# A dense value product for prompt tiles 1 and 2 of a product-key expert layer, with the expert value table read once

## The chip, the cores and the metric

The program runs on 1 core of one Trainium2 chip. Its time is the device time of one execution in microseconds, the median of several runs. Before the change it is 2445.83 us, the median of 3 runs.

## What is computed

The kernel is one decoder layer for a prompt of 512 tokens (with 16 meta tokens ahead of it) and 64 sample tokens (8 sequences of 8, each over 2048 cached keys). It projects, attends in two ways (a sparse attention with an indexer, and a forgetting attention), merges, normalises, and then runs the expert layer that the change is about. All data is float32.

```python
# peer, for one token x (1024 values), 8 heads, two sets of 128 keys a head
experts = ...            # 8 x 16 numbers in 0..16383, = 128*row + column, the best key pairs
gate = softmax(top)      # over the 16 of a head
pre = einsum('thkd,td->thk', expert_u[experts], x)
coef = gate * gelu(pre)
return einsum('thk,thkd->td', coef, expert_v[experts])
```

So each token needs its own 128 rows of `expert_u` and its own 128 rows of `expert_v`, both tables of 16384 rows of 1024 values (4 KB a row, 67 MB a table). After it, `x = LN2(ALPHA * h + PEER(h))`.

## The kernel before

Everything is written for the five engines by hand, with semaphores. The first 450 us or so are the projections and the prompt's attention. After them all engines follow one list, `plan`, built in Python: 1152 row gathers in a fixed order, and every other piece of work put at the number of a gather (`put(n, ...)`). Each engine walks through the list in order and does its own pieces, so a wait in one piece holds up everything that the same engine has behind it in the list.

Tokens come in five tiles: tiles 0 to 3 are prompt tiles of 128 tokens, tile 4 is the 64 sample tokens. A gather is an indirect DMA of GpSimd (line 918) that brings 128 table rows (512 KB) into one row buffer.

- U gathers (key rows, `expert_u`). One brings one expert row for each of a tile's 128 tokens, so a prompt tile needs 128 of them, and tile 4, packed two picks at a time, 64. VectorE multiplies the buffer with the tokens' h and sums (line 2081), which gives one column of `pre`.
- V gathers (value rows, `expert_v`). One brings the 128 rows of one token. TensorE multiplies them with the token's 128 coefficients, which ScalarE has laid into a strip (`add_rows`, line 1369): two matmuls of 512 columns with a 32-column stationary operand. The token's place in the strip decides its output row. A prompt tile has four such 32-column lanes, which TensorE can work at together when four tokens' rows are there (a `sum` of size 4). Each matmul is two instructions in the trace, since it is float32. Sums of one token stand where V gathers alternate with U gathers.

The order of gathers before: U of tile 0 (128), 72 V of tile 0, U of tile 1 mixed with the other 56 V of tile 0, then U of tiles 2, 3 and 4 mixed with V of earlier tiles, and last V of tile 4 (64). There are 10 row buffers (`NR0`), and 16 from gather 790 on. A gather waits for the product or sum that last read its buffer.

Beside the gathers the list carries: the routing of each tile on VectorE (16 steps of `route`, the best 16 keys and pairs a head), `gelu` and `coefs`, two merges (TensorE with weights that SyncE loads), and the sample attention: `ix`, `iy` (indexer products over pages that SyncE loads), `admit`, 32 rounds of `top` on VectorE (lines 1967 and 1968, 8 keys a round), and eight quarters `s_score`, `s_max`, `s_exp`, `s_turn`, `s_weigh`, `s_out` over cached keys and values (84 MB, SyncE's queue, a ring of four 1 MB slots). Before, `ix` starts at gather 199, `admit` stands at 276, the last `s_out` at 744, and the last merge ends at 840. At a tile's end `finish` adds the sums to h and `y_end` normalises.

## Time and profile before

| | |
|---|---|
| time, median of 3 runs (lowest to highest) | 2445.83 us (2444.44 to 2457.82) |
| span of the profiled execution | 2493.9 us |
| mean granted TensorE clock | 0.853 of full |
| bytes read from HBM | 784.13 MB |
| gathers | 576 of U and 576 of V rows, 604.58 MB |
| busy: TensorE, VectorE, GpSimd | 73%, 57%, 52% |

The profiled execution has no time of its own beside its span, 2493.9 us, which lies 48 us above the median of the plain runs (a factor of 0.981). Shares of busy time are means over stages that have different limits, so they say little about what a change in one stage is worth. "Idle before" in a group is the time in which the engine stood still just before such an instruction.

### The profile page before, as it was taken

Reading aid. Unit: us, or ns where it says so; the run is one execution under the profiler, and the core shown is the slowest. Engines: PE = TensorE matmul, PEld = TensorE weight load, DVE = VectorE, ACT = ScalarE, POOL = GpSimd, SP = SyncE. Lnnn points to the kernel's source line nnn. Section 1 sums busy time; section 2 is a strip of 40 time slices with the busy share of each in tenths; the row PEclk is TensorE's granted clock in tenths of the full one; section 3 lists DMA queues with packets and bytes.
Section 4 is the critical chain, followed back from the end, with each engine's and each line's share of the span. In section 5 each row is a group of like instructions: output and inputs, shape, how many; then the busy total and the mean of one; then the engine's idle time right before and its main releaser. Section 6 shows DMA issues by size and latency. Waiting matters only on the chain.

```text
span 2493.9 us, 23573 instructions
## 1 busy us (share of the span) xinstructions
PE 1810.2 (73%) x7244; PEld 768.0 (31%) x7247; DVE 1433.9 (57%) x3191; ACT 307.8 (12%) x732; POOL 1307.8 (52%) x1175
## 2 busy tenths in 40 slices
PE   9999988899699635566666766776777884555566
PEld 6767646644244201111112121221223250110011
DVE  2115876898845643999856569854444437434400
ACT  0214442111011101001101010110110010000000
POOL 1100000467655744555555557766777747677664
PEclk9998987999899867777778789998999997876678
DMA  5206322999989976999999999999999999999997
GB/s 182 71 3 195 102 85 68 355 328 410 361 306 368 346 281 238 394 367 400 386 401 380 401 371 362 371 356 368 378 384 409 409 370 374 364 359 380 355 377 287
DMA packets 259648, 791.92 MB, mean 318 GB/s; under 512 B 31522, under 2 KB 56163, under 8 KB 258947
## 3 DMA queue, kind: packets, MB, share of 16 engines
q0 software_dynamic: 166400, 604.58, 63.6%
q1 hardware_dynamic: 91268, 180.82, 20.6%
q10 hardware_dynamic: 1856, 5.03, 0.5%
q8 instruction: 58, 0.95, 0.2%
q14 instruction: 66, 0.54, 0.1%
HBM read 784.13 MB, written 5.59 MB: 317 GB/s over the span
## 4 chain that ended last, share of the span: by engine, by line
POOL 13%; DMA 10%; PE 8%; issue 7%; SPq 7%; another core or an unknown queue 6%; DVE 2%; ACT 1%; POOLq 0%
POOL arena L918 13%; DMA arena<-v_b 4%; PE ps L1369 3%; SPq L841 3%; DMA arena<-peer_v,arena 3%; SPq L768 2%; DMA arena<-peer_u,arena 2%; PE ps L1325 2%; DMA arena<-kv_a 2%; SPq L834 1%; PE ps L1202 1%; DVE arena L2081 1%; PE ps L1302 1%; ACT arena L1640 0%
## 5 line engine op out<-in xcount | busy, mean ns | idle before, releaser
L1369 PE MATMUL ps<-arena 128*32 128x512 f32 x2304 | 767.5, 717 | 346.6 <-DMA arena<-peer_v,arena 287.9
L2081 DVE CUSTOM_DVE_ANT_0 arena<-arena 128x1024 f32<-128x1024 f32 x576 | 694.7, 1225 | 531.5 <-DMA arena<-peer_u,arena 475.7
L918 POOL DMA_INDIRECT arena<-peer_v,arena x576 | 623.4, 1082 | 445.9 <-PE ps L1369 245.0
L918 POOL DMA_INDIRECT arena<-peer_u,arena x576 | 664.1, 1153 | 311.8 <-issue 162.2
L1369 PEld LDWEIGHTS ps<-arena 128*32 128x32 f32 x2304 | 153.4, 122 | 877.7 <-issue 662.1
L1164 PE MATMUL ps<-arena 128*128 128x448 f32 (+2 forms) x512 | 156.8, 467 | 13.1 <-DVE arena L1997 12.4
L1202 PE MATMUL ps<-arena 128*128 128x384 f32 (+2 forms) x704 | 146.5, 368 | 10.0 <-ACT arena L1576 8.1
L1325 PE MATMUL ps<-arena 128*64 128x512 f32 (+1 forms) x512 | 102.6, 538 | 68.1 <-DMA arena<-v_b 57.3
L900 POOL MEMSET arena<- 128x1024 f32 x1 | 1.0, 953 | 282.4 <-ACTq L723 282.4
L950 PE MATMUL ps<-arena 128*128 128x296 f32 (+1 forms) x512 | 132.1, 419 | 6.2 <-DMA arena<-xT 6.2
L1699 ACT ACTIVATE arena<-arena 128x8 f32<-128x8 f32 x72 | 15.3, 216 | 943.1 <-PE ps L1369 635.2
L1202 PEld LDWEIGHTS ps<-arena 128*128 128x128 f32 x704 | 104.3, 202 | 58.9 <-issue 26.8
L1164 PEld LDWEIGHTS ps<-arena 128*128 128x128 f32 x512 | 89.0, 193 | 87.0 <-issue 70.4
L950 PEld LDWEIGHTS ps<-arena 128*128 128x128 f32 (+1 forms) x512 | 96.9, 190 | 39.7 <-issue 8.3
L1284 PE MATMUL ps<-arena 128*32 128x512 f32 x256 | 51.6, 901 | 61.3 <-DMA arena<-k_b 61.0
L1325 PEld LDWEIGHTS ps<-arena 128*64 128x64 f32 x512 | 39.7, 159 | 144.0 <-issue 143.2
L895 POOL DMA_INDIRECT arena<-logf_b,arena x16 | 14.6, 913 | 126.4 <-PE ps L950 113.6
L2088 DVE SCALAR_TENSOR_TENSOR arena<-arena,ps 128x1024 f32<-128x1024 f32 (+1 forms) x5 | 6.1, 1219 | 126.2 <-PE ps L1369 84.6
L1967 DVE MAX8 arena<-arena 64x8 f32<-64x2056 f32 x32 | 73.6, 2299 | 1.0
L979 PE MATMUL ps<-arena 64*128 64x384 f32 (+9 forms) x168 | 69.9, 525 | 4.9 <-ACT arena L1545 1.9
L1968 DVE MATCH_REPLACE8 arena<-arena 64x2056 f32<-64x2056 f32 x32 | 73.1, 2286 | 0.0
L1825 DVE MAX8 arena<-arena 128x8 f32<-128x128 f32 (+3 forms) x120 | 34.2, 325 | 58.6 <-ACT arena L1583 53.2
(211 smaller groups left out, 1694.1 us busy)
## 6 DMA issues: line engine op xcount, KB each, us to landing
arena<-k_b SPq DMA_DIRECT2D x128, 256.0 KB
arena<-v_b SPq DMA_DIRECT2D x128, 256.0 KB
arena<-w_mix SPq DMA_DIRECT2D x56, 512.0 KB
arena<-w_q SPq DMA_DIRECT2D x48, 512.0 KB
arena<-kv_a SPq DMA_DIRECT2D x128, 128.0 KB
arena<-w_out SPq DMA_DIRECT2D x24, 512.0 KB
arena<-peer_u,arena POOLq DMA_INDIRECT x576
arena<-peer_v,arena POOLq DMA_INDIRECT x576
```

The lines of the kernel that those rows point to most:

```text
L841: sp.dma_start(ring[s_][:, j * 256:(j + 1) * 256], io["kv_a"][bass.ds(nos[j], 1)].rearrange("o p n -> (o p) n")).then_inc(ring_loaded[s_], 16)
L918: pool.indirect_dma_start(out=rows[slot_of[n]], out_offset=None, in_=io["peer_v"] if v else io["peer_u"], in_offset=bass.IndirectOffsetOnA ...
L950: last = pe.matmul(bank(2 * (m % 2) + a, HT, 0, n), wring[m % 3][:, k, 0:n], xT[:, k, a * HT:(a + 1) * HT], start=(k == 0), stop=(k == KD ...
L979: last = pe.matmul(out, heads[0:rows_, q, q0:q0 + nq], heads[0:rows_, kt, c0:c1], start=True, stop=not biased)
L1164: last = pe.matmul(out, mw_k[u % NMW][:, k0 + k, :], src[:, k, :], start=(k == 0), stop=(k == nk - 1))
L1202: last = pe.matmul(bank(4 + n % 2, WIDTH[p]), mw_k[u % NMW][:, k, :], hT[p][:, k, :], start=(k == 0), stop=(k == KD - 1))
L1284: last = pe.matmul(out[32 * lane:32 * lane + 32], qs_flat[:, at + 32 * lane:at + 32 * lane + 32], kk[e][:, :, hp, :], start=(hp % 2 == 0), ...
L1325: last = pe.matmul(out[e], probT_s[:, c, j * 128 + 64 * e:j * 128 + 64 * e + 64], rhs, start=(c == 0 and j == 0), stop=False)
L1369: last = pe.matmul(bank(6 + a, 512, 32 * lane, 32 * lane + 32), strips[:, GT * (G % 2) + k % GT, MID - r_:MID - r_ + 32], rows[slot_of[n]] ...
L1967: step(dve.max(top8, isamp))
L1968: step(dve.match_replace(isamp, top8, isamp, TAKEN))
L2081: dve.tensor_tensor_reduce(out=row, in0=row, in1=h, scale=1.0, scalar=0.0, op0=ALU.mult, op1=ALU.add, accum_out=pre[:, k:k + 1]).then_inc( ...
```

## The change

`expert_v` is no longer gathered row by row for tiles 1 and 2 (256 tokens). Instead a dense coefficient matrix is made and the whole table goes through TensorE once.

- Build. An expert's number is 128*i + j. For each token, VectorE makes two one-hot arrays out of the 128 picks (which lie on the partitions): 128 columns for j, and 64 columns for i with the coefficient multiplied in. TensorE multiplies the two, which gives the token's coefficients W[j, i] for 64 of the 128 i. ScalarE copies them into `w_dense`. A build is 4 tokens: three VectorE operations, 4 matmuls of 64 columns, one copy. There are 64 builds for each half of i, 128 in all.
- Dense. For each i, SyncE loads 128 consecutive table rows (512 KB, ring of 4 buffers, 128 loads in all), and TensorE multiplies with W[:, i, :] of both tiles: 4 matmuls of 512 columns with a 128-column stationary operand, accumulated in four PSUM banks over all 128 i.
- The list. 896 gathers instead of 1152: U0 (128), all of V0 (128), U1, U2, U3 (128 each), U4 mixed with half of V3 (128), the rest of V3 (64), V4 (64). 10 row buffers throughout. The sample stage is pressed together: its gaps are multiplied by 0.43 (`SAMPLE_PACE`), those of the last merge by 0.8. Now `ix` starts at gather 198, `admit` and the first scores stand at 231, the first 30 or so `top` rounds stand between 232 and 333, the last `s_out` at 432, the last merge ends at 501. The first 64 builds stand at 517 to 564, 64 dense pieces at 565 to 692, 64 builds at 694 to 742, 64 dense pieces at 742 to 869. Tiles 1 and 2 are finished at 873 and 883.
- The packing of tile 4 (four small DMAs behind waits, two before) moves from SyncE's queue to ScalarE's (`pack`, gather 626).

```diff
-        later = vs[1] + vs[2] + vs[3]
-        ALONE = 72
-        gathers = us[0] + vs[0][:ALONE] + weave(us[1], vs[0][ALONE:]) + weave(us[2], later[:120]) + weave(us[3], later[120:244]) + later[244:320]
-        gathers += weave(us[4], later[320:370]) + later[370:] + vs[4]
+        DENSE, BY_ROW = (1, 2), (0, 3, 4)
+        ALONE = 128
+        gathers = us[0] + vs[0][:ALONE] + weave(us[1], vs[0][ALONE:]) + us[2] + us[3]
+        gathers += weave(us[4], vs[3][:64]) + vs[3][64:] + vs[4]
...
+        SAMPLE_PACE, MERGE_PACE = 0.43, 0.8
...
-            at += gap
-        s_end = at
-        top_from, top_to = q_at_[("admit",)] + 2, q_at_[("s_out", 3)] + 24
+            at += SAMPLE_PACE * gap
+        s_end = int(at)
+        top_from, top_to = q_at_[("admit",)] + 1, q_at_[("s_out", 3)] + 8
...
+        BUILDS = 2 * 128 // GB
+        dense_items = [(("split",), 1.0)]
+        for h in range(2):
+            dense_items += [(("build", h, g), 1.3) for g in range(BUILDS)]
+            dense_items += [(("dense", h, e), 3.5) for e in range(HALF)]
+        d_from, d_to = max(m4_end + 2, turned_at[2] + 2), NG - 24
...
-            s_ = n % NR0 if n < SWITCH else (n - SWITCH) % NR
+            s_ = n % NR
...
+            def tables_of_values():
                 sp.wait_ge(sc_ready, 20)
+                for n in range(2 * HALF):
+                    if n >= NTB:
+                        sp.wait_ge(dense_used, n - NTB + 1)
+                    sp.dma_start(table[n % NTB], io["peer_v"][128 * n:128 * n + 128, :]).then_inc(table_loaded[n % NTB], 16)
...
+            def build(h, g):
...
+                pe.wait_ge(hot_ready, n + 1)
+                if n >= 2:
+                    pe.wait_ge(w_copied, n - 1)
...
+                for t in range(GB):
+                    last = pe.matmul(ps[:, c0 + HALF * t:c0 + HALF * (t + 1)], hot_j[n % NHOT][:, t, :],
+                                     hot_i[n % NHOT][:, t, :], start=True, stop=True)
...
+            def dense(h, e):
...
+                if e == 0:
+                    pe.wait_ge(w_copied, BUILDS * (h + 1))
+                pe.wait_ge(table_loaded[n % NTB], 16 * (n // NTB + 1))
+                for t in range(2):
+                    for a in range(2):
+                        last = pe.matmul(bank(2 * t + a), w_dense[t][:, e, :], table[n % NTB][:, a * 512:(a + 1) * 512],
+                                         start=(n == 0), stop=(n == 2 * HALF - 1))
...
+            def build(h, g):
...
+                if n >= NHOT:
+                    dve.wait_ge(w_built, n - NHOT + 1)
+                o_j, o_i = hot_j[n % NHOT], hot_i[n % NHOT]
+                dve.tensor_tensor(o_j, const("iota")[:, None, :].to_broadcast([128, GB, 128]),
+                                  col_no[t][:, t0:t0 + GB, None].to_broadcast([128, GB, 128]), ALU.is_equal)
+                step(dve.tensor_tensor(o_i, const("iota")[:, None, HALF * h:HALF * (h + 1)].to_broadcast([128, GB, HALF]),
+                                       row_no[t][:, t0:t0 + GB, None].to_broadcast([128, GB, HALF]), ALU.is_equal))
+                dve.tensor_tensor(o_i, o_i, coefD[t][:, t0:t0 + GB, None].to_broadcast([128, GB, HALF]), ALU.mult
+                                  ).then_inc(hot_ready, 1)
```

The order of instructions shows the change at three places. Rows that begin with L are in the order of one engine; ISA on VectorE is the row product.

First TensorE where the sample stage starts, before. L1236 and L1249 are `ix` and `iy`, L1369 is value sums (32 wide), L1284 the first scores:

```order
L1236 MATMUL ps<-arena 128x512 x4
L1369 MATMUL ps<-arena 32x512 x8
L1249 MATMUL ps<-arena 64x512 x2
L1369 MATMUL ps<-arena 32x512 x20
L1236 MATMUL ps<-arena 128x512 x4
L1369 MATMUL ps<-arena 32x512 x8
L1236 MATMUL ps<-arena 128x512 x4
L1249 MATMUL ps<-arena 64x512 x2
L1369 MATMUL ps<-arena 32x512 x6
L1347 MATMUL ps<-arena 128x128
L1369 MATMUL ps<-arena 32x512 x4
L1236 MATMUL ps<-arena 128x512 x4
```

The same place now (L1271 and L1284 are `ix` and `iy`, L1404 value sums, L1319 the scores):

```order
L1404 MATMUL ps<-arena 32x512 x8
L1271 MATMUL ps<-arena 128x512 x4
L1284 MATMUL ps<-arena 64x512 x2
L1404 MATMUL ps<-arena 32x512 x16
L1271 MATMUL ps<-arena 128x512 x4
L1284 MATMUL ps<-arena 64x512 x2
L1271 MATMUL ps<-arena 128x8 x4
L1404 MATMUL ps<-arena 32x512 x8
L1284 MATMUL ps<-arena 64x512 x2
L1284 MATMUL ps<-arena 64x8 x2
L1319 MATMUL ps<-arena 32x512 x8
```

The index products stand closer together, with fewer value sums, and so fewer gathers, between them.

Second VectorE in the first builds, which are new. L2225, L2227 and L2229 are one build, between the row products of tile 3 (ISA) and tile 4's routing (L1922 and on):

```order
L2179 ISA arena<-arena 128x1024
L2179 ISA arena 128x1
L2225 TENSOR_TENSOR arena<-arena 128x512
L2227 TENSOR_TENSOR arena<-arena 128x256
L2229 TENSOR_TENSOR arena<-arena 128x256
L2225 TENSOR_TENSOR arena<-arena 128x512
L2227 TENSOR_TENSOR arena<-arena 128x256
L2229 TENSOR_TENSOR arena<-arena 128x256
L2179 ISA arena<-arena 128x1024
L2179 ISA arena 128x1
L1922 MAX arena<-arena 64x8 x2
L1924 MAX_INDEX arena<-arena 64x8 x2
```

Four builds come to every three row products here.

Third TensorE from the first builds on, now (L1420 build, L1434 dense, L1404 value sums, L1386 and L1382 transposes of coefficients and numbers). Before, the end of its order was value sums alone, but for three transposes:

```order
L1386 MATMUL ps<-arena 128x128
L1420 MATMUL ps<-arena 128x64 x256
L1434 MATMUL ps<-arena 128x512 x16
L1382 MATMUL ps<-arena 128x128
L1434 MATMUL ps<-arena 128x512 x140
L1386 MATMUL ps<-arena 128x128
L1404 MATMUL ps<-arena 32x512 x4
L1434 MATMUL ps<-arena 128x512 x8
```

Where U and V gathers alternate, a value sum of two tokens now stands behind two dense pieces (8 matmuls).

## Rows read from the trace of the kernel before

**Rows 1.** Part 1 of the page.

```profile
PE 1810.2 (73%) x7244; PEld 768.0 (31%) x7247; DVE 1433.9 (57%) x3191; ACT 307.8 (12%) x732; POOL 1307.8 (52%) x1175
```

**Rows 2.** Busy time by stretch, start:end and length, busy us, clock, DMA share, GB/s.

```profile
core 0: us, PE busy (x) PEld busy (x) DVE busy (x) ACT busy (x) POOL busy (x), PEclk, DMA share, GB/s
995.00:1460.00 465.00, 299.50 (x1042) 82.18 (x1033) 364.20 (x613) 46.70 (x91) 260.19 (x226) 0.77 1.02 388
1460.00:1830.00 370.00, 257.58 (x829) 65.38 (x830) 226.65 (x508) 43.59 (x98) 256.68 (x219) 0.92 0.99 370
1830.00:2185.00 355.00, 250.35 (x1107) 95.43 (x1109) 177.59 (x461) 26.36 (x67) 240.03 (x224) 0.88 1.00 383
2185.00:2494.00 309.00, 172.33 (x589) 38.53 (x581) 90.60 (x146) 7.64 (x25) 201.13 (x203) 0.75 0.93 352
```

**Rows 3.** The row gathers alone (line 918) by stretch; (x) counts them.

```profile
829.00:995.00 166.00, 86.72 (x80) 0.71 0.80 282
995.00:1460.00 465.00, 260.19 (x226) 0.77 1.02 388
1460.00:1830.00 370.00, 256.68 (x219) 0.92 0.99 370
1830.00:2494.00 664.00, 441.15 (x427) 0.82 0.96 369
```

**Rows 4.** SyncE's queue in order of time, 128 index pages: start, us, what.

```profile
781.09 193.94 SPq L821 DMA_DIRECT2D arena<-kidx  x128
```

**Rows 5.** TensorE in order of time: last index products, idle before in brackets.

```profile
976.72 6.00 PE L1236 MATMUL ps<-arena 128*128 128x512 f32 x8 [20.93 <-DMA arena<-kidx]
993.21 0.40 PE L1249 MATMUL ps<-arena 128*64 128x8 f32 x4
```

**Rows 6.** VectorE, groups by shape: count, busy us, mean ns, idle before.

```profile
L2081 DVE CUSTOM_DVE_ANT_0 arena<-arena 128x1024 f32<-128x1024 f32 x576 | 694.7, 1225 | 531.5 <-DMA arena<-peer_u,arena 475.7 <-issue 48.5
L1967 DVE MAX8 arena<-arena 64x8 f32<-64x2056 f32 x32 | 73.6, 2299 | 1.0
L1968 DVE MATCH_REPLACE8 arena<-arena 64x2056 f32<-64x2056 f32 x32 | 73.1, 2286 | 0.0
L1981 DVE TENSOR_REDUCE arena<-ps 128x1 f32<-128x2056 f32 x8 | 18.4, 2295 | 8.3 <-PE ps L1277 8.3
L1854 DVE TENSOR_TENSOR arena<-arena 128x512 f32<-128x512 f32 x32 | 22.4, 701 | 1.1
L1839 DVE TENSOR_TENSOR arena<-arena 128x256 f32<-128x256 f32 x32 | 12.1, 422 | 6.9 <-ACTq L723 4.7 <-remote 1.8
```

**Rows 7.** VectorE in order of time: two row products back to back.

```profile
559.26 1.22 DVE L2081 CUSTOM_DVE_ANT_0 arena<-arena 128x1024 f32<-128x1024 f32 x1
560.41 1.22 DVE L2081 CUSTOM_DVE_ANT_0 arena<-arena 128x1024 f32<-128x1024 f32 x1
```

**Rows 8.** Busy time in two stretches, columns as in rows 2.

```profile
720.00:825.00 105.00, 102.84 (x534) 51.94 (x536) 57.83 (x246) 13.54 (x31) 57.65 (x62) 1.00 0.98 359
900.00:1000.00 100.00, 38.84 (x98) 11.53 (x96) 31.12 (x65) 6.30 (x14) 40.12 (x39) 0.69 0.68 235
```

**Rows 9.** TensorE, groups of instructions by shape.

```profile
L1369 PE MATMUL ps<-arena 128*32 128x512 f32 x2304 | 767.5, 717 | 346.6 <-DMA arena<-peer_v,arena 287.9 <-issue 48.5 <-DVE arena L2088 9.5
L961 PE MATMUL ps<-arena 128*128 128x512 f32 x64 | 28.1, 592 | 0.0
L1202 PE MATMUL ps<-arena 128*128 128x64 f32 x256 | 31.4, 281 | 0.4 <-DMA arena<-w_q 0.4
```

**Rows 10.** TensorE in order of time: value sums of 2, 1 and 8 tokens.

```profile
1165.49 1.92 PE L1369 MATMUL ps<-arena 128*32 128x512 f32 x8
1203.40 1.91 PE L1369 MATMUL ps<-arena 128*32 128x512 f32 x4
...
2044.05 3.67 PE L1369 MATMUL ps<-arena 128*32 128x512 f32 x32
```

**Rows 11.** Line 1178 on TensorE: shortest/median/longest ns, first and last start.

```profile
L1178 PE MATMUL ps<-arena x128: 592/592/1057, 615.8 to 1976.9; 128*128 128x512 f32 x96, 128*64 128x512 f32 x32
```

More of the change, by code:

```diff
@@ L283, in program @@
         coefT = [r.take(128) for _ in range(2)]
+        idsD, coefD = [r.take(128) for _ in range(2)], [r.take(128) for _ in range(2)]
         GT, SW, MID = 8, 64, 31
         strips = r.take(2 * GT, SW)
-        NR0, NR = 10, 16
+        NR = 10
         assert r.at <= tmp_at - (NHEADS - QI) * T
-        rows = [r.take(D) for _ in range(NR0)]
+        rows = [r.take(D) for _ in range(NR)]
         b_at = r.at
@@ L478, in program @@
         sums, sum_of = [], {}
-        for i in range(5):
+        for i in BY_ROW:
             for k in range(0, TOKENS[i], 4):
@@ L1404, in _ @@
                     add_rows(*at)
+                elif kind == "build":
+                    build(*at)
+                elif kind == "dense":
+                    dense(*at)
         @block.scalar
```

178 lines of the change are left out of this document (127 added, 51 removed).

## The prediction

> **What bounds the kernel now.** I read the page's busy shares first [rows 1]: no engine is above 73% over the span, so the limit changes with the stage. Then the busy time by stretch [rows 2]. From 995 us on the DMA share is 0.93 to 1.02 in every stretch at 352 to 388 GB/s, while TensorE is busy 56 to 71%. So transfers set the pace in the last 1500 us, and the reader should see that VectorE is filled only from 995 to 1460 (364 of 465 us), where the sample's key selection lies. The gather counts [rows 3] date the list: 200 gathers were issued by 829 us (1152 less 952), 280 by 995, 506 by 1460, 725 by 1830. The exception is 829 to 995: 80 gathers, and 235 GB/s from 900 on [rows 8]. There TensorE waits for index pages, which SyncE's queue issues one by one, 128 in 194 us from 781 on [rows 4]; TensorE stood 20.9 us before the last batch, and the last index product ends at 993.6 [rows 5].
>
> As a check, 445 gathers of 0.524 MB and some 80 MB of caches at 380 GB/s make 824 us, against 835 from 995 to 1830; 427 gathers and 17 MB of weights at 369 make 652 against 664 after it, with about 12 us of end.
>
> **The change, part by part.** Unit costs first.
>
> Transfers: 256 gathers go (134 MB), 128 table loads of 0.524 MB come (67 MB), so 67 MB less, 179 us at 375 GB/s. One such load, or a gather, is 1.36 us at 388 GB/s.
>
> VectorE: a row product costs 1.15 us back to back [rows 7], a top round 2.30 + 2.29 and gaps = 4.7, a sample maximum 2.3 [rows 6], the routing of a tile 58 us (busy time from 720 to 825 us, which holds nearly all of tile 1's 16 steps and little else [rows 8]), say 60. A build is one float32 tensor-tensor of 512 and two of 256: 701 + 422 + 422 = 1545 ns [rows 6]; back to back I take 1.5 us, 192 for 128 builds. Broadcast operands are in the 512 row too, so bounds are 1.4 and 1.7.
>
> TensorE: a dense piece is 4 matmuls, 8 instructions. 64 instructions of that shape were busy 28.1 us [rows 9], 0.44 each, so 3.5 a piece and 448 for 128. In a build, 8 instructions of 64 columns cost 31.4 / 256 = 0.12 each [rows 9], 1.0 a build. Value sums: one token alone 1.91, two together 1.92, eight in two fours 3.67 [rows 10], so 1.9, 0.96 and 0.46 a token. The 767.5 us of sums [rows 9] fall to 128 + 64 tokens in fours and 128 in pairs, some 210. All of these are for the high clock.
>
> ScalarE's copies (256 columns) and the packing cost nothing: ScalarE is busy 12% [rows 1] and has about 1.5 us a build. Without that cover each copy would add about 0.4 us to a build, 50 in all.
>
> Up to gather 198 nothing that matters moves. **The index pages** stay where they are in time: SyncE's queue issues them at its own pace. But now the last index products stand at gathers 226 to 230, not 264 to 274, and value sums behind them hold the 10 buffers. So at 995 us about 232 gathers have been read instead of 280, a loss of some 45 gathers, and VectorE has had nothing to do, since all of them are V. From there I add stretches, each at its slowest engine.
>
> - Gathers 232 to 333 (four quarters with 512 KB pages): VectorE 77 products 89, 30 top rounds 142, 12 routing steps 45, maxima 9, the rest 10 = 295. Transfers: 101 gathers 137, 63 MB of caches 162 = 299. Both are full and hand over to each other through 10 buffers and 4 slots; I take 320.
> - 333 to 517: VectorE 184 products 212, routing 20 steps 75, 2 rounds, maxima, merge and norms 57 = 344. Transfers 250 + 34 MB, 87 = 337. I take 344.
> - 517 to 565, 64 builds: VectorE 48 products 55, builds 96, 7 routing steps 26, rest 2 = 179. Transfers only 71, TensorE 64.
> - 565 to 640: transfers 75 gathers and 37 loads = 152, TensorE 130, VectorE 122. 155.
> - 640 to 694: TensorE 27 pieces 95, 27 tokens in pairs 26 = 121.
> - 694 to 742, 64 builds: VectorE 96 + 24 products 28 = 124; TensorE 87.
> - 742 to 768: TensorE 13 pieces 46 + 12 = 58.
> - 768 to 872: TensorE 51 pieces 179, 64 tokens in fours 29, 40 in pairs 38 = 246; transfers 155 x 1.36 = 211.
> - 872 to the end: 24 gathers 33 and 17 for the last sums and norms = 50.
>
> The sum is 1597, so the span is 995 + 1597 = 2592 us, 98 above before. Times 0.981 that is 2542 for the plain time; I forecast 2545.
>
> What goes right is the removed transfer, but it was the cover for VectorE and TensorE, and what is late next is these two: mostly U gathers up to 640 make VectorE the pace (labelled above), where before U and V alternated; and 660 us of TensorE work then stand in line behind the first builds. Bounds: with perfect overlap inside each half, VectorE needs 295 + 344 + 179 less 20 = 798 up to gather 565, and TensorE after that 448 + 64 + 64 + 64 of sums and builds and 17 of end, about 660. 995 + 798 + 660 = 2453, plain 2406, is the floor if the order holds. With 7% more for hand-overs in all stretches the span is 2704, plain 2652.
>
> **Rivals.**
>
> *Transfers stay the limit.* 2494 - 179 = 2315, plain 2270. For it: the DMA share of 1.0 [rows 2], and buffers that could smooth the rest. Against: the 45 lost gathers, and VectorE's 818 us from gather 232 to 565 where transfers need 707 (299 + 337 + 71); it decides only if that work of VectorE falls below 707.
>
> *Perfect packing.* The stretches overlap as far as the floor allows: plain 2406 to 2455. It needs TensorE never to wait from 565 on. Before, it waits in every stretch; 10 buffers hold 14 us of gathers, less than any stretch is long.
>
> *TensorE at its low clock.* The granted clock is 1.00 where TensorE is busy 98% and 0.69 where it is busy 39% and stands before transfers [rows 8]; instructions of 512 columns take 592 ns at 2.4 GHz and up to 1057 at 1.2 [rows 11]. From 517 to 565 TensorE is busy a third. If half of the work from 640 on (425 us, without the build stretch) ran at 1.2 GHz, that adds 0.5 x 425 x 0.79 = 168: 2760, plain 2707. For it: each dense piece waits for a load, each V sum for a gather. Against: once in the dense pieces TensorE is busy 80 to 100%, and the ring of four loads runs ahead. It decides if TensorE stands between the pieces as it stands between sums in [rows 2], where the clock was 0.75 to 0.92.
> The Trainium skill, page "TensorE: Matmul & The Clock Gate", section "HAM oscillation — how this bites in real kernels", says that a kernel whose matmuls for one piece are shorter than the wait for the next piece starts cold each time. Here a piece (3.5 us) is longer than its load (1.36), so by this rule the dense pieces stay warm; the rows of the stretch from 829 to 995 agree in the other direction.
>
> *The change doesn't do what it says.* If the number of transferred bytes did not fall by 67 MB, the time would come out as forecast all the same, since transfers set only 155 us of the sum. I give it nothing of its own.
>
> **How the numbers follow.** The forecast case, each stretch at its slowest engine, 0.64, with 2480 to 2640 as its own range; low clock 0.16, 2640 to 2740; perfect packing 0.10, 2406 to 2455; transfers the limit 0.10, about 2270. The predicted time is 2545. The range that leaves out no more than 2 in 10 is 2435 to 2680: it takes in the forecast, most of packing's upper part and part of the low clock. A measurement of this kernel can tell about 0.5%, 12 us, from no change. Faster than 2434: transfers and half of packing, 0.14. Within 12 us: 0.05. Slower than 2458: 0.81.
>
> **What would show it.** In the profile after: about 230 gathers issued by 990 us, with GB/s falling from 840 us on; VectorE above 95% busy from about 1000 to 1800 us but for hand-overs in the first 320; in the first builds a DMA share of 0.4 and TensorE at a third; after them TensorE above 85% to the end at a clock above 0.9, dense instructions near 0.44 each; HBM read near 717 MB. The forecast is wrong if VectorE shows gaps of more than 10% between 1320 and 1840 us, if a build costs under 1.2 or over 2 us, if gather 565 is read before 1760 us, or if the dense pieces take 5 us or more.

## The result, and the profile after

The kernel after takes 2661.41 us (median of 4 runs, 2655.76 to 2664.55), beside 2451.82 us (2444.44 to 2492.32) for the kernel before in the same comparison: a ratio of 1.084 [1.079, 1.089]. It is 210 us slower; I had forecast 2545, some 100 us slower. Some executions of the kernel before are about 40 us longer than its others (one of the four here, 2492.32 us; two of seven on chip 11, 2495 and 2499 us), and the comparisons on chip 11 below leave those two out, which makes its median there 2456.08 us.

First part 1 of the page, as in [rows 1], and its lines on bytes:

```profile
PE 1988.5 (75%) x8271; PEld 1086.6 (41%) x8271; DVE 1596.8 (60%) x3583; ACT 369.6 (14%) x820; POOL 1054.7 (40%) x919
HBM read 717.08 MB, written 5.59 MB: 272 GB/s over the span
```

The bytes fell by 67 MB as announced, and no engine's mean share of work (TensorE's weight loads aside) rose by more than three points. Only the stretches tell the story. Busy time by stretch, columns as in [rows 2], of a span of 2660.9 us:

```profile
829.00:995.00 166.00, 73.18 (x331) 21.94 (x327) 18.52 (x19) 11.27 (x27) 43.70 (x45) 0.68 0.66 223
995.00:1305.00 310.00, 157.76 (x682) 53.03 (x674) 264.27 (x425) 39.98 (x73) 107.73 (x94) 0.71 0.94 344
1305.00:1740.00 435.00, 188.09 (x931) 132.66 (x931) 331.26 (x760) 57.24 (x127) 248.92 (x188) 0.59 0.87 313
1740.00:1915.00 175.00, 124.27 (x515) 114.00 (x516) 171.47 (x416) 39.31 (x65) 54.67 (x49) 0.50 0.52 156
1915.00:2070.00 155.00, 138.92 (x320) 59.77 (x318) 123.87 (x292) 4.45 (x10) 98.12 (x76) 0.94 0.98 384
2070.00:2187.00 117.00, 117.00 (x336) 45.76 (x335) 39.50 (x70) 2.45 (x7) 53.05 (x53) 0.99 0.96 351
2187.00:2307.00 120.00, 104.51 (x573) 71.94 (x572) 109.98 (x228) 37.87 (x66) 52.56 (x46) 0.79 0.61 201
2307.00:2661.00 354.00, 330.68 (x1084) 118.88 (x1084) 34.61 (x49) 6.54 (x24) 140.12 (x147) 0.97 0.88 315
```

Where [rows 2] show a DMA share near 1 from 995 us to the end, three kinds of stretch now follow each other. In 829 to 995 nothing is full (VectorE 18.5 us of 166). From 995 to 1740 transfers and VectorE take turns, and in 1305 to 1740 neither is filled (331 of 435, and 0.87). From the first build at 1743 on TensorE, or in the builds VectorE, sets the pace (171 of 175, 117 of 117, 331 of 354), and the DMA share falls to 0.52 and 0.61 where the builds are. Only in 1915 to 2070, with a DMA share of 0.98 at 384 GB/s, are transfers full once more, as forecast.

The units, VectorE and TensorE groups by shape, beside [rows 6, 9]:

```profile
L2225 DVE TENSOR_TENSOR arena<-arena 128x512 f32<-128x512 f32 x128 | 88.1, 688 | 12.0 <-PE ps L1420 11.5
L2227 DVE TENSOR_TENSOR arena<-arena 128x256 f32<-128x256 f32 x128 | 53.7, 419 | 0.0
L2229 DVE TENSOR_TENSOR arena<-arena 128x256 f32<-128x256 f32 x128 | 54.8, 428 | 4.4
L1434 PE MATMUL ps<-arena 128*128 128x512 f32 x1024 | 457.0, 601 | 1.4 <-issue 0.7 <-ACT arena L1785 0.7
L1404 PE MATMUL ps<-arena 128*32 128x512 f32 x1280 | 241.8, 657 | 27.7 <-DMA arena<-peer_v,arena 25.4 <-issue 1.5 <-PE ps L1271 0.5
L1420 PE MATMUL ps<-arena 128*128 128x64 f32 x1024 | 195.6, 365 | 69.4 <-DVE arena L2229 66.7 <-issue 2.7
```

Builds cost VectorE 197 us (forecast 192), dense pieces 457 (448), value sums 242 (210). Only the builds on TensorE cost clearly more, 196 against 128: the clock stood at 0.50 in the first 64. All of this is TensorE's tail: 815 us of work in the last 918.

Dating the stretches by the gathers' numbers gives the comparison with the forecast's list. Each length runs from one gather's issue to another's, ten gathers late, since ten buffers lie between issue and use:

| gathers | forecast, us | measured, us |
|---|---|---|
| start of the sum (gather 232 read) | 995 | 991 |
| 232 to 333 | 320 | 328 |
| 333 to 517 | 344 | 426 |
| 517 to 565 (64 builds) | 179 | 173 |
| 565 to 640 | 155 | 148 |
| 640 to 694 | 121 | 122 |
| 694 to 742 (64 builds) | 124 | 127 |
| 742 to 768 | 58 | 62 |
| 768 to 872 | 246 | 242 |
| 872 to the end | 50 | 43 |

The span came out 69 us above the forecast's 2592, and one stretch holds more than all of it: 333 to 517, by 82 us. The other part of the miss is the factor of 0.981, by which I turned a span into a plain time, worth 50 us.

### The profile page after: what moved, and what is told of

It reads as the page before. It is cut to its first block and busy times, and to the rows that moved or that the text cites. A ratio compares the mean times of both kernels' runs of the same rounds, so it can differ in the third digit from the quotient of the medians.

```text
span 2660.9 us, 26069 instructions
## 1 busy us (share of the span) xinstructions
PE 1988.5 (75%) x8271; PEld 1086.6 (41%) x8271; DVE 1596.8 (60%) x3583; ACT 369.6 (14%) x820; POOL 1054.7 (40%) x919
## 5 line engine op out<-in xcount | busy, mean ns | idle before, releaser
L953 POOL DMA_INDIRECT arena<-peer_u,arena x576 | 718.2, 1247 | 661.6 <-DVE arena L2179 487.7
L953 POOL DMA_INDIRECT arena<-peer_v,arena x320 | 316.2, 988 | 515.9 <-PE ps L1404 440.6
L1434 PE MATMUL ps<-arena 128*128 128x512 f32 x1024 | 457.0, 601 | 1.4 <-issue 0.7
L1434 PEld LDWEIGHTS ps<-arena 128*128 128x128 f32 x1024 | 191.4, 191 | 265.8 <-issue 264.9
L1404 PE MATMUL ps<-arena 128*32 128x512 f32 x1280 | 241.8, 657 | 27.7 <-DMA arena<-peer_v,arena 25.4
L1420 PE MATMUL ps<-arena 128*128 128x64 f32 x1024 | 195.6, 365 | 69.4 <-DVE arena L2229 66.7
L1420 PEld LDWEIGHTS ps<-arena 128*128 128x128 f32 x1024 | 182.5, 273 | 99.1 <-DVE arena L2229 79.7
L1237 PE MATMUL ps<-arena 128*128 128x384 f32 (+2 forms) x704 | 171.0, 418 | 12.8 <-ACT arena L1637 4.5
L1237 PEld LDWEIGHTS ps<-arena 128*128 128x128 f32 x704 | 129.0, 251 | 55.3 <-issue 16.9
L1199 PEld LDWEIGHTS ps<-arena 128*128 128x128 f32 x512 | 100.0, 223 | 117.8 <-issue 100.8
L1404 PEld LDWEIGHTS ps<-arena 128*32 128x32 f32 x1280 | 51.1, 115 | 180.4 <-issue 178.7
L1327 PE MATMUL ps<-arena 128*64 128x512 f32 x64 | 28.7, 992 | 118.8 <-DMA arena<-kv_a 92.8
L1785 ACT ACTIVATE arena<-ps 128x256 f32<-128x256 f32 x128 | 78.9, 616 | 235.0 <-PE ps L1420 234.0
L2225 DVE TENSOR_TENSOR arena<-arena 128x512 f32<-128x512 f32 x128 | 88.1, 688 | 12.0 <-PE ps L1420 11.5
```

The source lines that it names most:

```text
L953: pool.indirect_dma_start(out=rows[slot_of[n]], out_offset=None, in_=io["peer_v"] if v else io["peer_u"], in_offset=bass.IndirectOffsetOnA ...
L1199: last = pe.matmul(out, mw_k[u % NMW][:, k0 + k, :], src[:, k, :], start=(k == 0), stop=(k == nk - 1))
L1237: last = pe.matmul(bank(4 + n % 2, WIDTH[p]), mw_k[u % NMW][:, k, :], hT[p][:, k, :], start=(k == 0), stop=(k == KD - 1))
L1327: pe.matmul(out[64 * e:64 * e + 64], qas_flat[:, 192 * e:192 * e + 64], kv[e][:, :, 0:128], start=True, stop=False)
L1404: last = pe.matmul(bank(6 + a, 512, 32 * lane, 32 * lane + 32), strips[:, GT * (G % 2) + k % GT, MID - r_:MID - r_ + 32], rows[slot_of[n]] ...
L1420: last = pe.matmul(ps[:, c0 + HALF * t:c0 + HALF * (t + 1)], hot_j[n % NHOT][:, t, :], hot_i[n % NHOT][:, t, :], start=True, stop=True)
```

## Experiments

The runs lie on several chips, and the kernel before is not equally fast on them: about 2400 us on four (chips 0, 3, 4 and 7), 2446 us on the chip of the result and 2456 us on chip 11. The kernel after was run on three: 2661 us on the first, 2653 us on chip 11 and 2627 us on chip 7. That last one, "after on chip 7" below, is set beside the kernels of chips 0, 3 and 4 too, since the kernel before takes the same on all four. So kernels are compared on one chip, or by the length of a stretch between two gathers.

**The kernel before, again.** No edit.

> The kernel before, unchanged, to read a second trace of it. The first trace had a span of 2493.9 us beside plain runs of 2444 to 2458, the trace of the changed kernel 2660.9 beside plain runs of 2656 to 2665. If profiling lengthens a run by 2%, this trace is again near 2494 and the factor 0.981 of the prediction stands. If the first trace was of a slow execution, this one is near 2446 and the factor was wrong: 50 us of the miss.

2402.81 us, beside a median of 2400.03 on that chip; its span is 2400.8, so span and time differ by 2 us. The stretch that had 282 GB/s and 80 gathers for [rows 3]:

```profile
829.00:995.00 166.00, 99.92 (x223) 22.40 (x225) 106.73 (x208) 10.30 (x22) 116.86 (x95) 0.81 1.04 378
```

Here the index pages went out in 150 us and held nothing up: a DMA share of 1.04, and VectorE busy 107 us. So the wait for index pages in [rows 3, 5] is not a fixed property of the kernel. Whether it came with that execution or with its chip is not shown: the two traces are of different chips. The 48 us between that trace's span and the median did belong to the execution: it is as long as the run of 2492.32 us. The factor of 0.981 compared one long execution with others that were 48 us shorter, and it was wrong to apply it to the kernel after: that one's span of 2660.9 stands beside a plain 2662.68 for the same execution.

**Were SyncE's many small loads the cause?** The 32 loads of 128 KB of a quarter (4 to 7) become four of 1 MB, of consecutive pages instead of pages by their numbers, so that these quarters compute with the wrong pages:

```diff
-                        for j in range(8):
-                            sp.dma_start(ring[s_][:, j * 256:(j + 1) * 256],
-                                         io["kv_a"][bass.ds(nos[j], 1)]...).then_inc(ring_loaded[s_], 16)
+                        sp.dma_start(ring[s_].rearrange("p (n c) -> p n c", n=8),
+                                     io["kv_a"][n0:n0 + 8].rearrange("n p c -> p n c")).then_inc(ring_loaded[s_], 16)
```

> The changed kernel, with each slot of the last four sample quarters loaded by one DMA of 1 MB from consecutive pages of the cache instead of eight of 128 KB by page number (the last four quarters attend to the wrong pages). Theory: the stretch from gather 333 to 517 took 426 us instead of 344 because a quarter's 32 loads take 21 to 35 us of SyncE's queue and can only start when the quarter before has freed the slots, so that TensorE, and behind it VectorE's maximum and the row products, stand. Then 50 to 85 us go: 2580 to 2610. Rival: the chain of maximum, exponent and transposes of a quarter, or the merge behind it, is what takes the time: under 25 us go, 2636 or more.

2638.86 us, 12 above after on chip 7, and 333 to 517 took 425 us, where it took 426 in after and 419 in after on chip 7. SyncE's queue in order of time (start, us, what), first after:

```profile
1378.76 29.26 SPq L883 DMA_DIRECT2D arena<-kv_a  x32
1437.19 35.36 SPq L883 DMA_DIRECT2D arena<-kv_a  x32
```

and with one load a slot:

```profile
1360.17 19.29 SPq L882 DMA_DIRECT2D arena<-kv_a  x4
1417.79 20.26 SPq L882 DMA_DIRECT2D arena<-kv_a  x4
```

The quarters start 58 us apart in both, although the four loads are issued in 19 to 20 us and the 32 in 29 to 35. The number of loads is not what matters; the rival's figure, 2636 or more, held.

**Was the table's own transfer the cause?** The four table buffers are loaded once and read 32 times, which leaves out 65 MB:

```diff
-                for n in range(2 * HALF):
-                    if n >= NTB:
-                        sp.wait_ge(dense_used, n - NTB + 1)
+                for n in range(NTB):
...
-                pe.wait_ge(table_loaded[n % NTB], 16 * (n // NTB + 1))
+                pe.wait_ge(table_loaded[n % NTB], 16)
```

> The changed kernel, with only the first four blocks of the value table loaded and used 32 times each (124 loads, 65 MB, left out). Theory: transfers set the pace only in the stretch from gather 565 to 640, so 10 to 35 us go: 2626 to 2651. Rival: transfers are the limit after gather 565 too, where they carry 97% of DMA time in places: 65 MB at 375 GB/s, 150 us or more go, 2510 or less.

2624.37 us (2613.28 to 2634.72), beside 2627.18 for after on chip 7. From gather 527, where the builds begin, to the end it took 903 us, where after on chip 7 took 914: 9 us of it in 565 to 640 and 5 in 640 to 694. So 65 MB more or less is worth some 10 us: transfers do not set the end of this kernel.

**The order of tile 0's value rows.** 72 alone and 56 among tile 1's key rows, as before the change (`ALONE = 72`).

> The changed kernel with the V rows of tile 0 in the old place: 72 of them alone, 56 mixed into tile 1's U rows. Theory: the number of gathers read by 995 us is set by the index products at gathers 226 to 230 and stays near 232, but 22 of them are now U, so VectorE has 25 us less to do later: 10 to 30 us go, 2631 to 2651. Rival: V rows alone were what left VectorE idle before 995 us and their order decides: 50 us or more go. Other rival: 56 sums of one token at 1.9 us instead of fours at 0.46 make TensorE late and it gets slower.

2615.25 us, 12 below after on chip 7. Gather 242 is issued at 951 us, where after on chip 7 has 963 and the two kernels before this one, on this chip, 977 and 975. That VectorE gets something to do from the few key rows among the index products would explain it, but was not tried by itself. The change's "all 128 value rows ahead" costs only this.

**The kernel after again, and the cost of the one-hot arrays.** In the second kernel VectorE makes them only for the first three builds, and TensorE multiplies what lies there:

```diff
+                if n >= NHOT:
+                    dve.memset(o_i[:, 0, 0:8], 0.0).then_inc(hot_ready, 1)
+                    return
```

> The changed kernel, unchanged, beside the others of this call, since the kernel before took 2400 us in the last call and 2445 in the first. Theory: the changed kernel is bound by VectorE and TensorE from 995 us on and hardly by transfers, so what makes the kernel before 45 us faster there gives it 10 to 25 us: 2635 to 2655. Rival: it gains the same 45 us, 2615 or less, and one load a slot, one read of the table and 72 V rows alone gained nothing.

> The changed kernel, with VectorE making the one-hot arrays for the first 3 builds only and one small memset in the place of the other 125 (all else stays, TensorE multiplies old arrays). Theory: VectorE's 1.5 us a build is the pace of both build stretches; 517 to 565 falls from 173 to about 85 us, 694 to 742 from 127 to about 95: 110 to 130 us less than the changed kernel beside it. Rival: TensorE's builds, at a clock of 0.50, are the pace there, and under 60 us go.

2653.21 and 2566.84 us on one chip, 86 less: between the theory's 110 and the rival's 60. The two stretches of builds, 48 gathers each, fall from 173 to 117 us and from 123 to 85. Busy time near them:

```profile
1725.00:1837.00 112.00, 99.83 (x460) 97.83 (x459) 79.29 (x255) 33.09 (x58) 56.25 (x47) 0.50 0.75 255
2115.00:2203.00 88.00, 88.00 (x573) 61.18 (x572) 29.70 (x105) 34.30 (x59) 55.34 (x48) 1.00 0.91 319
```

The first window begins some 20 us ahead of the first build, in the merge; over the 64 builds themselves, 1746 to 1861 us, TensorE was busy 110 of 115 us. So VectorE did set the pace of the builds, and TensorE is next in line, at 96% and 100%; that is why not all 192 us come back. Even with the arrays for nothing the kernel is slower than before, 1.043 [1.038, 1.049].

**The pressed sample stage alone.** The kernel before, all rows gathered, with the stage's gaps multiplied by 0.43 and the merge's by 0.8. Two things move along with it: the last `top` rounds stand 8 instead of 24 gathers behind the fourth `s_out`, as in the change, and the step from 10 row buffers to 16, which the list puts behind the stage's end, comes at about gather 470 instead of 790 (worked out from the gaps), where the kernel after has 10 throughout.

```diff
-            at += gap
-        s_end = at
-        top_from, top_to = q_at_[("admit",)] + 2, q_at_[("s_out", 3)] + 24
+            at += 0.43 * gap
+        s_end = int(at)
+        top_from, top_to = q_at_[("admit",)] + 1, q_at_[("s_out", 3)] + 8
```

> The kernel before, with no dense product, but with the sample stage pressed to 0.43 and the last merge to 0.8 as in the change. Theory: pressing alone costs the transfers of some 45 gathers while TensorE waits for index pages (60 us where the stall is as in the first trace, less where pages come sooner) and up to 40 us in the last four quarters, which stand on their loads: 40 to 120 us over the kernel before. Rival: pressing is harmless by itself, within 10 us, and the whole loss is in the dense part.

2622.93 us, 167 above before's 2456.08 on that chip, 1.069 [1.061, 1.076], well over the 120 at the top of what I expected. The kernel after was 30 us further up on the same chip. So the two kernels lose nearly the same time, and a kernel that has no dense product at all loses it, although it has the 16 row buffers early. Its stretches:

```profile
829.00:995.00 166.00, 69.19 (x219) 20.68 (x219) 59.01 (x79) 11.96 (x25) 57.65 (x52) 0.72 0.71 245
1305.00:1550.00 245.00, 140.49 (x638) 51.75 (x637) 103.96 (x193) 40.79 (x92) 128.38 (x107) 0.76 0.86 306
```

In the second one VectorE is busy 104 us of 245, and transfers 0.86: again nobody is full over the whole of it.

**Only the index part at its old places** (and `ALONE = 72`, and the merge at 0.42 for room):

```diff
-            at += SAMPLE_PACE * gap
+            at += (SAMPLE_PACE if ("admit",) in q_at_ else 1.0) * gap
```

> The changed kernel with 72 V rows alone and the index products at their old gathers (last at 274, the first scores at 276 instead of 231); the rest of the sample stage keeps its gap of 0.43 and so ends 45 gathers later, and the last merge is pressed to 0.42. Theory: at 995 us some 276 gathers have been read instead of 232, among them 52 of U: 60 us of VectorE's work and 60 us of transfers lie ahead of that point. 45 to 70 us less than the changed kernel, 20 to 50 less than with 72 alone. Rival: VectorE idles later for the same time, and it ends with 72 alone's time or above it.

2612.12 us, 41 below after on the chip, a little under what I expected. Gather 242 is issued at 892 us, 96 earlier than in after on that chip, but gather 575 at 1878 beside 1914: more than half of the gain is gone again when the first builds end.

**Three parts of the stage pressed by themselves,** in the kernel before: up to `admit`, from there to the fourth `s_out`, and behind it. The second and third also have the last `top` rounds 8 instead of 24 gathers behind the fourth `s_out`.

```diff
-            at += 0.43 * gap
+            at += (1.0 if ("admit",) in q_at_ else 0.43) * gap                                # first
+            at += (0.43 if ("admit",) in q_at_ and not ("s_out", 3) in q_at_ else 1.0) * gap  # mid
+            at += (0.43 if ("s_out", 3) in q_at_ else 1.0) * gap                              # last
```

> The kernel before, where only the index pages' part of the sample stage (up to admit) has its gaps multiplied by 0.43; the rest follows 45 gathers earlier at its old gaps. Pressing the whole stage cost 159 us over the kernel before. Theory (the pages' queue needs its 194 us, and gathers that no longer stand between the index products are idle time until it is done): gathers 198 to 242 take 60 to 80 us more than in the kernel before, some of it is paid back later, and the time is 30 to 70 us over the kernel before. Rival (the loss is one of the whole stage, where each part alone has slack around it that absorbs it): less than 20 us over. If the three partial presses add up, their sum is 130 to 190 us.

> The kernel before, where only the first half of the stage's attention (admit to the fourth s_out, with the 32 top rounds between) has its gaps multiplied by 0.43. Theory (VectorE has 147 us of top rounds there beside 1.2 us for every key row, and the stage's share of gathers falls from 236 to 101): 30 to 70 us over the kernel before. Rival (slack absorbs it): less than 20 us. Second rival: this part holds the most of the 159 us, over 90.

> The kernel before, where only the second half (quarters 4 to 7 of the cached values) has its gaps multiplied by 0.43. Theory (a quarter's chain takes some 57 us and has about 25 gathers, 33 us at the pace of this kernel's DMA, to hide behind): four quarters by up to 24 us, less what comes back later, 30 to 80 us over the kernel before. Rival (the slots of the ring and the 10 row buffers are enough to hide it): less than 20 us.

2446.26, 2447.00 and 2437.27 us beside 2401.01, so 45, 46 and 36 above, ratios of 1.018, 1.018 and 1.016, each with an interval of 0.002 to either side. The sum is 127, below the 167 of all together on another chip. The loss is spread over the whole stage, and no part has slack enough of its own. The busy time where the first and the last stand:

```profile
829.00:995.00 166.00, 72.03 (x228) 20.38 (x227) 62.34 (x91) 12.48 (x25) 67.77 (x60) 0.73 0.74 261
```

```profile
1460.00:1830.00 370.00, 259.82 (x1187) 110.96 (x1186) 193.75 (x484) 49.30 (x118) 203.00 (x184) 0.86 0.92 344
```

**Room for the last four quarters within the new list:** their gaps at 0.66, the merge at 0.42.

```diff
-            at += SAMPLE_PACE * gap
+            at += (0.66 if ("s_out", 3) in q_at_ else SAMPLE_PACE) * gap
```

> The kernel after, with the gaps of quarters 4 to 7 of the cached values multiplied by 0.66 instead of 0.43, and those of the last merge by 0.42 instead of 0.8, so that the merge still ends before tile 4's routing. Theory (a quarter of this stage is a chain of load, scores, exponent, transposes and value product that takes some 57 us, and it sets the pace where the list gives it fewer gathers than that): gathers 333 to 517 take 426 us now and 365 to 400 here, and the time falls by 25 to 60 us against the kernel after, to 2595 to 2630 us. Rival (the stretch is bound by what has to be moved and multiplied in it, not by where the pieces stand): 415 to 430 us again, and 2640 to 2665 us. Second rival: the squeezed merge gives it all back, with 333 to 517 at 400 to 420 us.

Gathers 333 to 517 took 372 us, in after on chip 7 419, and the time is 2675.41 us: no gain at all, and 48 above after on chip 7. The theory held for the stretch and the second rival for the time, although not where it looked: 517 to 565 took 218 us, in after on chip 7 173. TensorE there, in order of time:

```profile
1699.12 13.92 PE L1237 MATMUL ps<-arena 128*128 128x64 f32 x64
1712.97 1.97 PE L1249 MATMUL ps<-arena 128*64 128x128 f32 x8
1714.87 13.92 PE L1237 MATMUL ps<-arena 128*128 128x64 f32 x64
```

The squeezed merge (L1237, L1249) is still being worked off, back to back at a granted clock of 0.50, and VectorE stands 36.4 us before it with the first builds behind it. The gathers also flatter the stage here: its last value product ended at 1584 us (1521 in after on chip 7) and the first build began at 1744 (1708). A quarter, from value product to value product, took 79, 71 and 67 us with 32 to 38 gathers beside it (58, 58 and 52 with 22 to 24 in after on chip 7), and TensorE stood 92.5 us before the cached pages, against 91.0. So a quarter is no fixed 57 us, as the theory had it: with more gathers beside it, it gets longer, and its waits stay.

**Room for the whole stage.** All value rows of tile 3 go ahead of tile 4's key rows, so that the merge may end 128 gathers later (first kernel), or half of them, 64 (second). The third has the first's room with `ALONE = 128`.

```diff
-        SAMPLE_PACE, MERGE_PACE = 0.43, 0.8
+        SAMPLE_PACE, MERGE_PACE = 0.72, 0.6
-        gathers += weave(us[4], vs[3][:64]) + vs[3][64:] + vs[4]
+        gathers += vs[3] + us[4] + vs[4]
```

> The kernel after itself, for comparison on the same chip: 2650 to 2665 us.

> The kernel after with room for the sample stage: all 128 value rows of tile 3 stand before tile 4's key rows, so tile 4's routing begins at gather 658 instead of 530; the sample stage's gaps are multiplied by 0.72 (0.43 in after) and the merge's by 0.6 (0.8), and 72 value rows of tile 0 stand alone, the other 56 among tile 1's key rows. The builds and the dense product then have gathers 651 to 872 (517 to 869 in after). Theory (the loss is that the sample stage's pieces stood closer than they can be done, and the dense product by itself costs little): gathers 198 to 651 take 880 to 960 us, which with 822 us before them is 1700 to 1780; behind them builds and dense pieces run at TensorE's and VectorE's pace, two halves of about 150 + 229 us, some 740 to 800 with the end: 2470 to 2560 us, 100 to 190 below after. Rival (the dense product needs the gathers of the longer stretch beside it, and what the sample stage gains is lost behind it): within 30 us of after.

> As the kernel with all of tile 3's value rows ahead of tile 4's key rows, but with only half of them ahead: tile 4's routing begins at gather 594, the sample stage's gaps are multiplied by 0.61 and the builds begin at gather 589. Theory: between the two, 60 to 130 us below after. Rival: within 30 us of after, or further below it than the other, if the dense product needs the gathers beside it.

> As the kernel with all of tile 3's value rows ahead of tile 4's key rows and the sample stage's gaps at 0.72, but with all 128 value rows of tile 0 alone ahead of tile 1's key rows, as in after. In after that order costs: with 72 alone the gathers before the stage's admit came earlier by 23 to 36 us. Theory (value rows among tile 1's key rows relieve VectorE while it does the top rounds): 20 to 50 us over the version with 72 alone. Rival (it matters only where the stage is pressed): within 10 us of it.

2627.18, 2671.92, 2655.01 and 2700.62 us on one chip (for the first I expected 2650 to 2665; it is another chip). My theory here, that more room for the stage would bring 100 us or more, fell. The gathers did come sooner: in the second kernel number 343 at 1144 us (1291 in the first) and 527 at 1558 (1709). But now look at the time ahead of the first build and behind it, after on this chip, and then the second kernel, 0.72 with `ALONE = 72`:

```profile
995.00:1708.00 713.00, 325.43 (x1537) 179.41 (x1530) 572.42 (x1175) 88.52 (x186) 348.07 (x273) 0.64 0.90 328
1708.00:2623.00 915.00, 808.72 (x2823) 405.28 (x2823) 477.25 (x1045) 90.63 (x170) 403.54 (x369) 0.87 0.81 287
```

```profile
995.00:1848.00 853.00, 396.42 (x1710) 195.42 (x1709) 674.70 (x1315) 101.88 (x211) 472.73 (x377) 0.66 0.92 341
1848.00:2672.00 824.00, 776.77 (x2789) 408.57 (x2789) 331.15 (x793) 89.86 (x162) 248.77 (x238) 0.87 0.68 238
```

The second has 104 gathers more between 995 us and the first build (and 28 more ahead of 995), which cost 140 us, and 131 fewer behind it, which save 91: there TensorE has 777 to 809 us of work whatever stands beside it, so the tail cannot shrink with the gathers, and the DMA share only falls to 0.68. The rival had it right. The value rows of tile 0 alone cost 29 us here (2700.62 less 2671.92), as the theory in that run had it.

**What stretches a quarter?** Quarters 5, 6 and 7 aren't loaded but compute with quarter 4's data:

```diff
-                        sp.wait_ge(slot_read, z - NSLOT + 1)
-                        for j in range(8):
+                        if q == 4:
+                            sp.wait_ge(slot_read, z - NSLOT + 1)
+                        for j in range(8 if q == 4 else 0):
```

> The kernel after, where the cached keys and values of quarters 5, 6 and 7 are not loaded (12.6 MB, 96 transfers) and these quarters compute with what quarter 4 left in the four slots; all their other work stands. Gathers 333 to 517 take 416 to 434 us in the kernel after in three traces. Theory A (a quarter's load can only start when the quarter before has read all four slots, so its time is part of a chain, and the load's 20 to 35 us cannot be hidden): three quarters lose 15 to 25 us each, the stretch falls to 350 to 380 us, the time by 40 to 70. Theory B (the transfers' sum is what counts there): 12.6 MB at the stretch's 280 to 300 GB/s, 42 to 45 us, likewise; it differs from A in the DMA share, which would be 0.9 or more in 1500 to 1700 us, while A leaves it below 0.85. Rival (VectorE's work and the exchange of scores, exponents and transposes set the quarter, not its load): the stretch stays at 400 us or more and the time falls by less than 20 us.

2579.56 us, 48 below after on chip 7, and 333 to 517 fell to 365 us, where after on chip 7 took 419: within what theory A gave. All of the 54 us lie in the quarters: from value product to value product they took 34, 34 and 46 us, where after on chip 7 took 58, 58 and 52. TensorE in after, in order of time, from one quarter's value product to the next:

```profile
1376.62 3.71 PE L1360 MATMUL ps<-arena 128*64 128x128 f32 x64
...
1399.29 1.98 PE L1327 MATMUL ps<-arena 128*64 128x512 f32 x4 [17.88 <-DMA arena<-kv_a]
...
1418.98 1.98 PE L1327 MATMUL ps<-arena 128*64 128x512 f32 x4 [15.13 <-DMA arena<-kv_a]
...
1434.62 3.72 PE L1360 MATMUL ps<-arena 128*64 128x128 f32 x64
...
1467.79 1.98 PE L1327 MATMUL ps<-arena 128*64 128x512 f32 x4 [25.78 <-DMA arena<-kv_a]
...
1491.31 3.68 PE L1337 MATMUL ps<-arena 128*128 128x128 f32 x16 [6.79 <-ACT arena L1708]
```

and the waits behind it in after from 1400 to 1700 us (total, times, longest), by waiting line and releaser:

```profile
POOL arena L953 <- DVE arena L2179: 106.1, 24, 23.9
PE ps L1327 <- DMA arena<-kv_a: 92.8, 6, 25.8
DVE arena L2078 <- PE ps L1312: 58.4, 3, 26.0
```

The reader should see a ring: the product at 1376.6 frees the four slots, the next quarter's 4 MB come in, scores follow at 1399 and 1419, maximum and exponent, transposes, and the next product at 1434.6. That is 58 us in this quarter, and 33 of them are waits for pages. VectorE stands before the maximum (L2078) up to 26 us, its row products behind it in the list; so the ten row buffers stay full, and GpSimd waits too. When the maximum is done the buffers come free, and gathers and page loads then go out together. Busy time of after in the first part of a turn and in the part in which the pages are awaited:

```profile
1410.00:1441.00 31.00, 13.31 (x101) 8.15 (x101) 16.42 (x28) 8.70 (x15) 10.92 (x8) 0.67 0.55 185
1441.00:1468.00 27.00, 0.90 (x4) 0.53 (x6) 13.28 (x22) 3.27 (x11) 18.77 (x16) 0.50 1.03 389
```

So transfers are half idle for 31 us, and then full for 27 us, in which TensorE does next to nothing: the 4 MB of pages share that time with 16 gathers (8.4 MB). Every engine and the transfers wait in turn. Busy time from 1400 to 1500 us, in after on chip 7 and then without the three loads:

```profile
1400.00:1500.00 100.00, 31.65 (x210) 17.17 (x210) 71.11 (x172) 20.38 (x46) 58.02 (x45) 0.59 0.84 300
```

```profile
1400.00:1500.00 100.00, 28.47 (x225) 20.45 (x223) 96.17 (x247) 18.83 (x40) 68.73 (x57) 0.63 0.94 349
```

VectorE goes from 71 to 96 us of 100 when the loads are gone. The DMA share from 1500 to 1700 us, by which I wanted to tell theory B (the sum of transfers) from A, came out at 0.87, between the two marks, and after on chip 7 has 0.94 there: that place lies behind the quarters and decides nothing. Two other figures speak against B. Over gathers 333 to 517 the share was 0.88 with the loads and 0.92 without, so it rose where B's limit was taken away. And 12.6 MB at the pace of full transfers there (320 GB/s by 0.88, 364) are 35 us, an estimate, where 54 went. That a quarter waits for the slots in a ring, and that this costs 54 us in three quarters, is shown; how much of it is the pages' own transfer beside the gathers, and how much their late start, is not.

## Why the prediction was right and wrong

**The direction and the large steps held.** Gathers removed from a kernel that transfers bound did take their cover off VectorE and TensorE. The bytes, the builds on VectorE, the dense pieces, and eight of the nine stretches (within 8 us each) came out as the list had them. The start at 991 us was right as well, and so was the shape: first builds with VectorE at 98%, then TensorE at 87 to 100%. In the first builds, though, TensorE was busy 126 of 174 us, not a third, since its clock was low.

**The step that failed is "333 to 517: VectorE ... 344. Transfers ... 337. I take 344."** It measured 426, and 419 on chip 7. VectorE was busy 331 us of 435 there, the gaps of over 10% between 1320 and 1840 us that the prediction itself named as the sign of being wrong. The two sums need not be wrong (with three quarters' loads taken away the stretch takes 365, and VectorE is at 96% in the part shown), but taking the larger of two engines' sums supposes that both may run ahead of each other. They may not where a quarter needs all four slots: load, scores, maximum, exponent, transposes and product then form one chain, measured at 52 to 61 us, with 25 gathers, some 34 us of transfer, to hide it. Of the 75 us over the forecast on chip 7, the loads of three quarters account for 54; the other 21 stay open. The list and [rows 3] could have warned me: before, the last four quarters stood 58 gathers apart, and at that stretch's pace (370 / 219 = 1.69 us a gather) that is 98 us, so the chain was hidden; pressed to 0.43 it no longer is. In the second trace of the kernel before a quarter took 78 to 89 us and TensorE stood 11 us before those pages in all four; with the last part pressed, 55 to 59 us and 52. I counted busy time, and not the length of the chain. The 7% for hand-overs that I allowed in the upper bound is far less than the 24% of this stretch.

**The factor of 0.981 failed too,** by 50 us. It stood on a span and plain times of different executions. [Rows 3, 5] show that execution waiting for index pages, and the same kernel on chip 3 does not. It could also not carry over: what varies from one execution or chip to the next is the pace of transfers (before differs by 54 us between chips 7 and 11), and a kernel bound by engines varies less (after by 26 between the same two).

**"The index pages stay where they are in time"** held by its result only. SyncE's queue issued them in 161 us here, not in 194, and the last index product ended at 960. Still the gathers were as far behind at 990 as I had counted, since the first scores come right behind, each before pages of its own.

**The rivals.** *Transfers stay the limit*: refuted, 65 MB fewer bring some 10 us. *Perfect packing*: refuted, no stretch came out more than 7 us below its own slowest engine's sum. *TensorE at its low clock*: true in the first builds, where the granted clock was 0.50, that is 1.2 GHz. Both build stretches together cost TensorE 68 us of busy time over the forecast's 128, but that made little of the whole, as VectorE was the slower there. It was not true of the dense pieces, which had 0.94 to 0.99 from 1915 to 2187 and stood before next to nothing (1.4 us in 1024 instructions). The rule that I cited from the Trainium skill ("TensorE: Matmul & The Clock Gate", section "HAM oscillation — how this bites in real kernels") agrees with the dense pieces. The builds it doesn't explain: from 1743 to 1917 TensorE worked 126 of 174 us and stood before VectorE 48 times, 54 us in all, so with 1.1 us a wait and 1.97 a build its pieces were mostly longer than its waits, and the clock stayed at 0.50.

**Whose loss is it?** Pressing the stage, with 16 buffers from about gather 470, costs 167 of the 197 us by which after stood over before on the one chip with both. The other 30 are what the dense part and the fewer buffers cost together, after 67 MB were saved; the two were not tried apart. But pressing and the dense part can't be had apart. The dense part needs the memory of the sample stage and tile 4's routing needs the merge, so either the stage is pressed, or its room is taken from the gathers that the dense part should run beside. The kernels with more room show the second way to be no better.

No version that was run beats the kernel before.

## What to carry to other kernels

When work is moved closer together, compare the length of its longest dependent chain, from the moment its buffer comes free to the moment it is free again, with the time that the new spacing gives it; sums of busy time by engine don't show it. That length is not a constant either: here a quarter took 52 to 61 us with some 23 gathers beside it and 67 to 79 with 32 to 38. A large piece of TensorE work takes the place of transfers only if it can stand beside them: if memory or order put it behind the stage that fills the DMA queues, bytes saved come back as a tail. And a correction factor between a span and a median is worth a second execution before it enters a sum.

## What the runs showed of the hardware

The same 64-column matmuls ran at two clocks in one kernel (that without one-hot arrays). From 1746 to 1861 us the granted clock was 0.50 (1.2 GHz), with TensorE busy 110 of 115 us, behind a merge of equally short matmuls at that clock. From 2115 to 2203 us it was 1.00 (2.4 GHz), with TensorE busy throughout, behind dense pieces of 512 columns and with value sums of 512 columns between the builds. And the kernel before differs by 2.3% from chip to chip (2401 and 2456 us), while the kernel after differs by 1.3% (2627 to 2661 us).
